# A two-layer mixture-of-experts decoder trunk on one core: the overflow branch moved ahead of the last up matrices, the first gather in pieces, and each layer's last weights, sums and stores by halves of the output columns

## The reference, cut to what matters

```python
# every layer: x += Mixer(RMSNorm(x)); x += HierMoE(RMSNorm(x))
g_sel = argmax(g_logits)                      # one of 4 groups
top_v, top_i = lax.top_k(e_in, 2)             # two of its 8 experts
gate = p_g * softmax(top_v)
a = silu(xb @ w_gate[e]) * (xb @ w_up[e])     # 1024 -> 512, 32 experts
y = a @ w_down[e]                             # 512 -> 1024
out = segment_sum(y[dest] * flat_w, tok)      # back to the tokens
```

## Time and profile before

| | us |
|---|---|
| median of 3 runs (lowest, highest) | 1213.78 (1213.77, 1214.67) |
| profiled execution, its own time | 1218.09 |
| its span | 1216.2 |
| TensorE matmul busy | 967.0 (80%) |
| VectorE, ScalarE busy | 213.3, 139.3 |
| moved | 447.27 MB, mean 368 GB/s |
| chain that ended last | DMA 50%, PE 47% |

### The profile page before, as it was taken

One profiled execution on the slowest core, in us unless ns is written; L12 is line 12 of the kernel. 1 busy time (PEld: TensorE's weight loads), 2 busy tenths in 40 slices (PEclk: granted clock), 3 DMA queues, 4 the chain that ended last, 5 costly groups with the idle time before them and its releaser, 6 DMA issues.

```text
span 1216.2 us, 11723 instructions
## 1 busy us (share of the span) xinstructions
PE 967.0 (80%) x5158; PEld 413.3 (34%) x5158; DVE 213.3 (18%) x455; ACT 139.3 (11%) x259; POOL 10.2 (1%) x11
## 2 busy tenths in 40 slices
PE   8999999767685858676789999996776757686767
PEld 7555554221222212131236655542121212121212
DVE  3812332010100000000025541410000000010101
ACT  3411211000000000000011330110000000000000
POOL 0000010000000000000000000000000000000000
PEclk9999999887888888787889999998878788887879
DMA  9782598999999999999995327899999999999995
GB/s 333 233 322 77 188 420 331 428 429 424 428 429 429 426 428 429 428 426 429 412 387 205 139 99 324 332 429 428 427 428 426 428 429 427 427 429 427 427 421 221
DMA packets 61892, 447.27 MB, mean 368 GB/s; under 512 B 13072, under 2 KB 13328, under 8 KB 39312
## 3 DMA queue, kind: packets, MB, share of 16 engines
q1 hardware_dynamic: 61840, 446.49, 88.9%
HBM read 445.43 MB, written 1.05 MB: 367 GB/s over the span
## 4 chain that ended last, share of the span: by engine, by line
DMA 50%; PE 47%; DVE 1%; issue 1%; ACT 0%; SPq 0%; DVEq 0%
PE psum L550 19%; DMA ring<-in_w_up 13%; PE psum L837 11%; DMA wide<-in_w_down 10%; DMA wide<-in_w_gate 10%; DMA ring<-in_w_down 5%; DMA wide<-in_w_up 5%; DMA ring<-in_w_gate 5%; PE psum L834 5%; PE psum L897 5%; PE psum L508 1%; PE psum L495 1%; DMA ring<-in_w_in_ab 1%; PE psum L911 1%; PE psum L483 0%
## 5 line engine op out<-in xcount | busy, mean ns | idle before, releaser
L550 PE MATMUL psum<-ring,mixed 128*32 128x512 f32 x1664 | 408.9, 714 | 120.3 <-DMA ring<-in_w_up 56.0
L550 PE MATMUL psum<-wide,mixed 128*32 128x512 f32 x1408 | 400.9, 713 | 106.9 <-DMA wide<-in_w_gate 63.1
L550 PEld LDWEIGHTS psum<-ring,mixed 128*32 128x32 f32 x1664 | 92.4, 128 | 323.6 <-issue 155.9
L550 PEld LDWEIGHTS psum<-wide,mixed 128*32 128x32 f32 x1408 | 88.0, 128 | 271.3 <-issue 124.4
L837 PE MATMUL psum<-ring,wide 128*128 128x512 f32 x320 | 140.3, 593 | 0.0
L837 PEld LDWEIGHTS psum<-ring,wide 128*128 128x128 f32 x320 | 59.6, 190 | 68.8 <-issue 68.4
L495 PE MATMUL psum<-y_sb,spread 128*128 128x512 f32 x144 | 66.6, 605 | 2.1 <-DVE y_sb L686 2.1
L508 PEld LDWEIGHTS psum<-sel,h 128*128 128x128 f32 x528 | 61.9, 196 | 15.4 <-issue 13.4
L508 PE MATMUL psum<-sel,h 128*128 128x128 f32 x528 | 65.4, 283 | 1.7 <-DVE sel L658 1.7
L681 DVE TENSOR_TENSOR mixed<-psum,sig 128x512 f32<-128x512 f32 x16 | 16.9, 1058 | 281.3 <-PE psum L550 281.3
L619 ACT COPY mixed<-psum 128x512 f32<-128x512 f32 x36 | 20.9, 586 | 347.5 <-PE psum L508 347.5
(11 more groups left out here) (247 smaller groups left out, 499.6 us busy)
## 6 DMA issues: line engine op xcount, KB each, us to landing
ring<-in_w_down SPq DMA_DIRECT2D x38, 2048.0 KB, 34.7
ring<-in_w_up SPq DMA_DIRECT2D x36, 2048.0 KB, 37.6
wide<-in_w_gate SPq DMA_DIRECT2D x34, 2048.0 KB, 36.8
ring<-in_w_gate SPq DMA_DIRECT2D x30, 2048.0 KB, 30.2
wide<-in_w_up SPq DMA_DIRECT2D x28, 2048.0 KB, 28.2
wide<-in_w_down SPq DMA_DIRECT2D x26, 2048.0 KB, 35.1
ring<-in_w_in_ab SPq DMA_DIRECT2D x8, 2048.0 KB, 14.7
ring<-in_w_in_cd SPq DMA_DIRECT2D x6, 2048.0 KB, 21.6
```

Source lines behind the costliest of these rows:

```text
L550: mm = pe.matmul(psum[slots, out + n, :], inp[:, c, slots], slot(layer, unit)[:, at + 512 * n:at + 512 * (n + 1)], start=c == 0, stop=c == ...
```

## The change

- The first gather of a layer goes in pieces. Chunks 0 and 1 go to bank YB+1 and chunks 2 and 3 to bank YB; ScalarE copies each pair by itself; the gate matrices start with chunks 0 and 1, and chunks 4 to 7 are gathered after the first quarter of the gate matrices (`quarterway`).
- The branch on overflow stands ahead of the last quad's up matrices; both arms hold up, gather, transposes and down (`up_and_down`).
- The last unit of a layer's weights comes as two loads, one for each half of the output columns (512 columns, 2 KB rows). The last down quarter, the copy of y, spread_back, the add and the final stores go by these halves. ScalarE copies both halves of the last y.
- ScalarE's and VectorE's loops over the quads go over 7, and the last is written out behind them.
- Layer 1 starts with the transposes of tc 0 alone; those of tc 1 come two steps into the first projection, and the square of tc 1 moves behind ScalarE's copies.

```diff
@@ load_expert_unit
+                if u == n_moe - 1:
+                    src = t["w_down"][layer, quad * TILE:(quad + 1) * TILE].rearrange("e (p c) n -> p e c n", c=rows)[:, :, rows - 1, :]
+                    n = expert_unit(layer, u)
+                    by_half = slot(layer, n).rearrange("p (b e n) -> p b e n", b=2, e=TILE)
+                    sp.wait_ge(S["unit_used"], unit_free(layer, n))
+                    for b, signal in enumerate((S["half_landed"], unit_landed[unit_place(layer, n)])):
+                        sp.dma_start(by_half[:, b], src[:, :, b * 512:(b + 1) * 512]).then_inc(signal, 16)
@@ stores
-            for tc in range(TC):
-                sp.wait_ge(S["finished"], TC + tc + 1)
-                sp.dma_start(out[:, tc, :], x[:, tc, :]).then_inc(S["stored"], 16)
+            for b in range(2):
+                for tc in range(TC):
+                    cols = slice(b * 512, (b + 1) * 512)
+                    sp.wait_ge(S["finished"], 4 + 2 * b + tc + 1)
+                    sp.dma_start(out[:, tc, cols], x[:, tc, cols]).then_inc(S["stored"], 16)
@@ moe_pe
+            def gather_rest():
+                gather_chunks(4, 8).then_inc(m["gathered"], 1)
+                pe.wait_ge(m["xT_ready"], 1)
-            gather()
+                gather_chunks(0, 2, YB + 1).then_inc(S["gather_begun"], 1)
+                gather_chunks(2, 4).then_inc(m["gathered"], 1)
                 pe.wait_ge(S["route_ready"], layer + 1)
                 count = pe.value_load(over_i[0:1, layer:layer + 1], min_val=0, max_val=SEQ)
...
-                matrix(i, 0, GATE, xT, KC, FF, halfway=lambda: pe.wait_ge(m["xT_ready"], (n17 + i) * 2 + 2))
+                matrix(i, 0, GATE, xT, KC, FF, halfway=lambda: pe.wait_ge(m["xT_ready"], (n17 + i) * 2 + 2),
+                       quarterway=gather_rest if first else lambda: None)
...
+            def last_half(n):
+                if n == 0:
+                    pe.wait_ge(S["half_landed"], 16 * (layer + 1))
+                else:
+                    wait_unit(pe, layer, expert_unit(layer, n_moe - 1))
+                for e in range(TILE):
+                    slots = slice(e * SLOTS, (e + 1) * SLOTS)
+                    at = n * HALF + e * 512
+                    mm = pe.matmul(psum[slots, YB + n, :], actT[:, FC - 1, slots],
+                                   slot(layer, expert_unit(layer, n_moe - 1))[:, at:at + 512], start=False, stop=True)
+                return mm
...
             with pe.Else():
-                last_quarter()
-                pe.wait_ge(m["y_ready"], 2 * (QUADS + 1))
-            for tc, signal in enumerate(("spread_first", "spread_second")):
-                spread_back(pe, tc).then_inc(m[signal], 1)
+                up_and_down(QUADS - 1, last=True)
+                keep_busy(pe, 3, UP, ident, ones)
+                last_half(0).then_inc(m["y_half"], 1)
+                pe.wait_ge(m["y_ready"], y_all - 1)
+                for tc in range(TC):
+                    spread_half(0, tc)
+                last_half(1).then_inc(S["unit_used"], 1)
+                pe.wait_ge(m["y_ready"], y_all)
+                for tc in range(TC):
+                    spread_half(1, tc)
@@ keep_gathered (ScalarE)
+                if first:
+                    act.wait_ge(S["gather_begun"], layer + 1)
+                    nc.scalar.copy(xT[:, 0:2, :], psum[:, YB + 1, 0:2 * P]...).then_inc(S["xT_begun"], 1)
+                    act.wait_ge(m["gathered"], 1)
+                    nc.scalar.copy(xT[:, 2:4, :], psum[:, YB, 2 * P:4 * P]...).then_inc(m["xT_ready"], 1)
@@ add_experts (VectorE)
+            for n in range(2):
+                for tc in range(TC):
+                    part_ = x[:, tc, 512 * n:512 * (n + 1)]
+                    dve.wait_ge(M[layer]["spread_done"], 2 * n + tc + 1)
+                    nc.vector.tensor_tensor(part_, part_, psum[:, ACC + 2 * tc + n, :], ALU.add).then_inc(S["finished"], 1)
@@ layer 1's start
-            for tc in range(TC):
-                turn_x_start(pe, 1, tc)
+            turn_x_start(pe, 1, 0)
-            project(1, 0, {8: (then(wait_hT, 1, False),), 12: (then(inverse_row, 1),)})
+            project(1, 0, {2: (then(turn_x_start, pe, 1, 1),), 8: (then(wait_hT, 1, False),), 12: (then(inverse_row, 1),)})
```

More of the change, by code:

```diff
@@ L490, in start_sums, with spread_back @@
                           skip_group_check=True)
-        def spread_back(pe, tc):
-            for n in range(2):
+        def spread_back(pe, tc, halves=(0, 1)):
+            for n in halves:
                 mm = pe.matmul(psum[:, ACC + 2 * tc + n, :], spread[:, tc, :], y_sb[:, 512 * n:512 * (n + 1)],
@@ L529, in over_matrix, with matrix @@
                     mm.then_inc(m["used"], 1)
-            def matrix(i, matrix, out, inp, rows, width, halfway=lambda: None, only_last=False):
+            def matrix(i, matrix, out, inp, rows, width, halfway=lambda: None, quarterway=lambda: None):
                 if over:
@@ L538, in matrix @@
                 last = (i, matrix) == (QUADS - 1, 2)
-                for c in range(rows - per if last else 0, rows) if only_last else range(rows - per if last else rows):
+                for c in range(rows - per if last else rows):
                     if c == rows // 2:
                         halfway()
+                    if c == rows // 4:
+                        quarterway()
                     if quartered and c % per == 0:
@@ L574, in quad, with up_and_down @@
                     spread_back(pe, tc)
+                if not last:
+                    up_and_down(i)
+            def up_and_down(i, last=False):
                 matrix(i, 1, UP, xT, KC, FF)
@@ L629, in moe_act @@
                 nc.scalar.copy(spread, psum[:, UP, 0:TC * P].rearrange("p (c s) -> p c s", c=TC)).then_inc(m["actT_ready"], 1)
-                wait_matrices(act, layer, rnd, i, 3)
+                if last:
+                    act.wait_ge(m["y_half"], 1)
+                else:
+                    wait_matrices(act, layer, rnd, i, 3)
                 nc.scalar.copy(y_sb[:, 0:512], psum[:, YB, :]).then_inc(m["y_ready"], 1)
+                if last:
+                    wait_matrices(act, layer, rnd, i, 3)
+                    nc.scalar.copy(y_sb[:, 512:1024], psum[:, YB + 1, :]).then_inc(m["y_ready"], 1)
+            keep_gathered(n17 + 1, first=not over)
+            with act.Fori(0, QUADS if over else QUADS - 1) as i:
+                act_quad(i)
+            if not over:
+                act_quad(QUADS - 1, last=True)
         def clear_outputs(layer):
@@ L684, in moe_dve @@
                 weighted(i + 1)
-                wait_matrices(dve, layer, rnd, i, 3)
-                nc.vector.tensor_copy(y_sb[:, 512:1024], psum[:, YB + 1, :]).then_inc(m["y_ready"], 1)
-        def add_experts(dve, layer):
[L690 to L693, removed]
+                if not last:
+                    wait_matrices(dve, layer, rnd, i, 3)
+                    nc.vector.tensor_copy(y_sb[:, 512:1024], psum[:, YB + 1, :]).then_inc(m["y_ready"], 1)
+            with dve.Fori(0, QUADS if over else QUADS - 1) as i:
+                dve_quad(i)
+            if not over:
+                dve_quad(QUADS - 1, last=True)
+        def add_experts(dve, layer):
+            for n in range(2):
+                for tc in range(TC):
+                    part_ = x[:, tc, 512 * n:512 * (n + 1)]
+                    dve.wait_ge(M[layer]["spread_done"], 2 * n + tc + 1)
+                    nc.vector.tensor_tensor(part_, part_, psum[:, ACC + 2 * tc + n, :], ALU.add).then_inc(S["finished"], 1)
         roots_asked, roots_taken = [], []
@@ L754, in begin_act @@
         def begin_act(act, turn, layer):
-            for tc in range(TC):
+            for tc in range(TC if layer == 0 else 1):
                 square(act, 2 * layer, tc)
@@ L762, in begin_act @@
             r.then_inc(S["hT_second"], 1)
+            if layer == 1:
+                square(act, 2, 1)
             take_root(act, turn)
```

73 lines of the change are left out of this document (43 added, 30 removed).

## The result

| | before | after |
|---|---|---|
| first comparison, median us (executions) | 1214.22 (4) | 1204.90 (4) |
| second | 1217.32 (17) | 1203.29 (6) |
| third | 1217.01 (17) | 1204.14 (6) |
| profiled execution, its own time | 1218.09 | 1203.57 |
| its span | 1216.2 | 1201.8 |

The ratio was 0.992 (95%: 0.9902 to 0.9937) in the first comparison, 0.9891 (0.9871 to 0.9912) in the second and 0.9893 (0.9869 to 0.9917) in the third. The change makes the kernel faster, by 9 us in the first comparison and by 13 to 14 us in the two larger ones. The time of 1204.9 is outside the forecast range (1196.5 to 1204.0); 1199.5 was too low by 3.8 to 5.4 us.

The account below looks back on a forecast made before the run. The prediction took TensorE and VectorE, then the weight stream, then TensorE with hand-overs as the bounds. Gains of 3.4 (stream starts), 6.1 (layer 0's tail) and 4.8 (layer 1's) made 14.3 us, giving 1199.5 us; range 1196.5 to 1204.

Parts of the forecast that it names:

- I take the difference off the median: Final step: the 14.3 us gain subtracted from the runs' median, 1213.78, though the profiled execution took 1218.09; gives 1199.5 us.
- the term of 15.48 us in layer 0: Old time from the third down quarter's end through spread_back in layer 0, including 4.45 us at the branch; forecast 8.8.
- the sum of 14.3: Total forecast gain in us: 3.4 from stream starts, 6.1 from layer 0's tail, 4.8 from layer 1's tail.
- Start of the stream: Splitting each layer's first gather frees a weight place earlier, so the DMA queue issues sooner: 1.7 us gain per layer.
- The loss of 0.2 us for the register read: Ahead of the first gate, the overflow register read has fewer gather instructions covering it; 0.2 us deducted from 1.9.
- Tail: Third down quarter's end to last spread_back: 8.8 us at full clock, gaining 6.7 in layer 0, 3.7 in layer 1.
- The rival of a falling clock: Hand-overs in the new tail lower TensorE's clock, costing 2.5 us per layer and 1 more: 1205.5 us; chance 0.10 less 0.01, stated 0.09.
- Branch: Ahead of the last up matrices, a 4.45 us branch is hidden in both layers, with 2.4 and 0.9 us to spare.
- a longer gap where transfers run at full rate: Reason for expecting 4.45 us or more at the branch's new place: old gaps of 4.45 and 2.63 under differing transfer.
- Landing of the halves: The last down unit's halves land before TensorE wants them, cover 0.7 and 1.6 us; rival of late landing, chance 0.05.
- Layer 1's start and the end: Moved transposes make layer 1's start 0.6 us worse; smaller final add and store gain 0.5 and 0.6 us.

Follow-up runs that it names:

- gather_only: The kernel before with only the first gather in pieces: 0.995 against the kernel before, 6.1 us faster.
- no_branch: The kernel before without the overflow rounds and without the branch on every engine: 0.9924 against the kernel before.
- a_third: The changed kernel, unaltered, timed and traced a third time: 0.9893 against the kernel before, 1204.14 us.
- branch_up: The kernel before with the overflow branch alone moved ahead of quad 7's up matrices: 0.993 against the kernel before, 8.5 us faster.
- b_again: The kernel before, unchanged, timed against itself and traced again: 0.9996.
- branch_mid: The kernel before with the branch between quad 7's up matrices and the gather of the filler chunk: 0.9969 against the kernel before, 3.8 us faster.
- a_no_fill: The changed kernel without the three fillers ahead of the last down unit's first half: 0.9862 against the kernel before, 1201.10 us.

## Why the prediction was right in its terms and wrong in its time

**The step that failed** is "I take the difference off the median". The sum was made from an execution of 1218.09 us and subtracted from a median of three executions at the lower end of before's scatter, 1213.78. The traced execution was near the usual one, the median was not: in four later comparisons it was 1216.94 to 1218.74, each of 17 to 26 executions. Against its own execution the sum gives 1203.8; the changed kernel's profiled one took 1203.57. Against before's usual time, 1217, it gives 1202.7, where 1203.3 to 1204.9 were measured. A difference of 4.3 us between trace and median, a third of the forecast gain, was seen and noted, but not asked for its place. Its place isn't known now either: the term of 15.48 us in layer 0, with its gap of 4.45, was nearly the same in the two later traces (gaps of 4.35 and 4.34), and no trace was taken of an execution near 1213.8. The two larger comparisons, with gains of about 10 to 16 us by their intervals, take in the sum of 14.3; whether a part of it is short by about 1 us is not shown.

**Start of the stream.** Right in mechanism and size: 1.8 us earlier at the queue in layer 0, and the last up matrix 1.8 us earlier in gather_only. In layer 1 it was 3.4 in the first trace, of which 1.6 is the clock of the gather (5.46 us to the gate against 3.84 in no_branch), which came out high there and low in a_third. The loss of 0.2 us for the register read did not show.

**Tail.** Right: 8.86 and 8.88 us against 8.8, and the granted clock was 1.00 in the fillers, halves and spread_backs of both layers. The rival of a falling clock is refuted by every trace of the changed kernel and by the two versions without fillers. TensorE's pauses there, 0.7 us for each copy, did not lower it.

**Branch.** Right that it is covered, wrong in the margin. I expected it as a gap of 4.45 us or more with 0.9 us to spare; the gap was 0 and 0.17 us (branch_up and no_branch agree within 0.1%). The reason given, a longer gap where transfers run at full rate, fell: b_again has 4.80 us in layer 1 at 86 GB/s, and branch_mid 2.60 and 2.58 us at 399 and 402 GB/s. "Runtime: NRT & Kernel Launch" of the Trainium skill (Instruction fetch mechanics) says that a taken branch whose target is not in the fetched window must wait for a DMA of it. The traces agree: a packet of 16 KB on an instruction queue in or at the edge of each gap of 2.0 to 4.8 us. At the new place the fetch was not avoided, it ran beside spread_back.

**Landing of the halves.** Right: TensorE never waited for them, and a_no_fill, which asks for half 0 some 1.5 us sooner, didn't either.

**Layer 1's start and the end.** Right within 0.1 us.

**The parts.** The sum hid that the halves alone give nothing (1.0011): they paid only with the branch out of the way.

## What to carry to other kernels

Subtract a sum made from a trace from the time of that traced execution, and when it differs from the median by a good part of the gain, find the term that varies before giving a range. A branch behind the last wait for weights showed as 2.1 to 4.8 us of idle TensorE; behind spread_back (3.7 us) and ahead of waits for landings it showed as 0.41 us at most in the changed kernel and cost nothing. Look at the instruction queue's packets to see when the fetch begins. Once a gap is gone, look at what it covered: here the fillers for the clock became pure cost, and the last landing came into sight.

## What was not expected of the hardware

The idle time at one and the same branch was 4.45, 4.35 and 4.34 us in layer 0 and 2.63, 4.80 and 2.79 us in layer 1 in three traces of one kernel. The first gather of layer 1, of the same instructions, took 5.46 or 5.47 us in six traces and 3.84 in two, of kernels that differ elsewhere. And code can be waited for twice: in branch_mid a second gap of 2.01 us came 4 us after the end of the first, where the profile shows no wait but again a packet on the instruction queue.
